# A Trainium2 MLP whose products of two neighbouring weight strips are issued alternately, into four PSUM banks, with the block loop written out

## The chip, the cores and the metric

The kernel runs on one core of a Trainium2 chip. The metric is the device time of one execution in microseconds (us), the median of several runs. The engines are named as in the profile: PE is TensorE (PEld its weight loads), DVE is VectorE, ACT is ScalarE, POOL is GpSimd, SP is SyncE, which here only issues DMAs.

## What is computed

One layer of a streaming encoder over 2048 prompt rows and 32 sample rows of 1024 channels: a normalised input projection, two branches (a recurrence and a banded attention), their merge into x, and then the MLP, which alone is changed. Cut to the MLP, the reference is:

```
D_MODEL = 1024; SEQ = 2048; DEC_SEQ = 32; D_FF = 4 * D_MODEL
...
    h2 = modulate(x, P["norm_mlp_g"][l], sh2, sc2)            # RMS norm, gain and shift
    x = x + g2 * (jnp.square(jax.nn.relu(h2 @ P["w_ff1"][l])) @ P["w_ff2"][l])
...
    y_prompt = rms_norm(xp, final_norm_g)
    y_sample = rms_norm(xs, final_norm_g)
```

All is float32. The kernel splits each float32 factor into a high part (type fp32r, which PE takes in one pass) and the rest, the low part, and adds three products for each: high by high, high weight by low activation, low weight by high activation.

## The kernel before

The stages run one after the other: modulation and first norm, projection and recurrence, attention, merge (`build_merge`), MLP (`build_mlp`). The MLP takes the 2080 rows in NB = 5 blocks of BW = 416 columns; a block is turned so that channels lie on partitions and the 416 rows are the moving columns of every product.

**Units.** A block has 64 units. Unit u uses one weight strip of 1024 by 128 floats (512 KB) and consists of 24 products of 128x128 by 128x416 into one PSUM bank: 8 slices of the contraction by the 3 products named above (`split_products`, L1609). Units 0 to 31 are the first layer: unit u makes 128 of the 4096 hidden channels. Units 32 to 63 are the second layer: output tile m (128 of the 1024 channels) takes four units in a row, q = 0 to 3, all into one bank, m = (u - 32) // 4. The banks `ff_ps0` and `ff_ps1` alternate by u in the first layer and by m in the second.

**Strips.** SP loads strip s into one of four buffers `ff_raw` (L2025) once the low part of strip s - 4 is made. ACT copies it into `ff_hi` (`make_hi`, L2004) once unit s - 2 is through on PE, DVE subtracts that from the strip into `ff_lo` (`make_lo`, L2008), and PE begins the unit when `ff_lo` is there. `ff_hi` and `ff_lo` have two buffers. PE marks a unit as through with the last of its 24 products (semaphore `ff_products`, called `mm_s` in the code).

**What else hangs on a unit.** ACT, DVE and PE each go through the units in the same order; what they do at unit u stands in their `body`, and each engine takes its instructions strictly in that order. In the first layer, once unit u is through, ACT takes the ReLU out of PSUM (L2046), DVE squares it (L2086), ACT and DVE split it (L2051, L2089). In the second layer, once a tile's last unit (q = 3) is through, DVE scales the sum and adds it to x (`x_now`, L2095, two pieces). Between the units stands work for the neighbouring blocks: `final_at(u)` lists the final norm and the output of the block before (squares at units 1 to 8, mean at 10, rows at 12 to 19, transposes and stores at 21, 23, 25, 27), `next_at(u)` the norm of the block that comes next (squares at 35 to 42, mean at 44, the normalised tiles h at 46, 48, ... 60). One tile h is a multiplication on DVE (L1941), the gain and shift and the copy to its high part on ACT (L1927, L1930), and the low part on DVE (L1945).

**The next block's input.** At unit 29 DVE copies the block's input from `x_next` to `x_now` (`move`, L2076, 1.9 us); this stands behind DVE's work on the square of unit 29. SP loads the input of the following block into `x_next` (1664 KB, L1908), and this load stands in SP's program between the loads of strips 32 and 33. It waits for that copy.

**Block loop.** Blocks 0 and 4 are written out; blocks 1 to 3 are a hardware loop (`each_block`, L2010), whose waits compare semaphores with register values.

## Time and profile before

| | us |
|---|---|
| time, median of 3 runs | 5020.41 (5019.88 to 5023.28) |
| span of the profiled execution (first to last instruction), its own time | 5024.5 |
| MLP in the profiled execution, from its first product to its last | 3463.7 to 4991.2 |
| PE busy in the whole span | 4518.3 (90%) |
| DVE, ACT busy in the whole span | 2050.3 (41%), 1480.1 (29%) |
| granted PE clock, mean of the span | 0.935 |

The profile is of one execution, and durations below are its. Matmuls are pipelined on PE and their ends are modelled, so a product's row shows 0.35 us although the next begins after 0.19 us: the distance between the starts of two products is the figure to read, and a unit's length is the distance between the starts of its first product and of the next unit's first. Idle time is shown with the engine and line that ended it.

### The profile page before, as it was taken

To read this page: it belongs to the slowest core of one execution; us is meant where nothing else is said; L and a number is where in the kernel's file an instruction comes from. 1 tells how busy PE (TensorE), PEld (TensorE's weight loads), DVE (VectorE), ACT (ScalarE), POOL (GpSimd) and SP (SyncE) were. 2 spreads that over 40 slices of the span, in tenths; PEclk is the share of its full clock that TensorE was granted. 3 is DMA by queue.
4 is the path that set the end of the run, shared out by engine and by line. 5 is a ranking of instruction groups with operands and counts; after the bars stand their busy time and mean duration, and the time that the engine had idled before them with its cause. 6 is when DMAs were issued, how large, how long until landed. Compare 5 with 4: busy or idle time off the path is not lost. (4 is left out here: it accounts for less than half of the span.)

```text
span 5024.5 us, 69286 instructions
## 1 busy us (share of the span) xinstructions
PE 4518.3 (90%) x25724; PEld 4165.4 (83%) x25724; DVE 2050.3 (41%) x3699; ACT 1480.1 (29%) x2543; POOL 574.0 (11%) x547
## 2 busy tenths in 40 slices
PE   6799899999999999865488878997999999999998
PEld 3599898999999999764366657997999999999997
DVE  3400344444444444443245544333435444353442
ACT  2311222222222222211134333123334344343432
POOL 1210222232222223221000000000000000000000
PEclk9899999999999999977569878998999999999999
DMA  6422111111111111000400004333434434344342
GB/s 223 149 72 69 43 37 38 47 36 36 44 40 36 36 47 37 24 10 7 147 9 8 8 29 156 109 105 102 129 111 118 126 109 137 110 122 123 109 127 81
DMA packets 595632, 390.45 MB, mean 78 GB/s; under 512 B 99313, under 2 KB 585353, under 8 KB 594449
## 3 DMA queue, kind: packets, MB, share of 16 engines
q1 hardware_dynamic: 528336, 309.63, 21.8%
q10 hardware_dynamic: 67136, 78.63, 4.4%
q8 instruction: 109, 1.79, 0.2%
q14 instruction: 51, 0.41, 0.0%
HBM read 306.86 MB, written 81.34 MB: 77 GB/s over the span
## 5 line engine op out<-in xcount | busy, mean ns | idle before, releaser
L522 PE MATMUL proj_ps<-h_hi,w_hi 128*128 128x416 f32 x1680 | 601.2, 358 | 14.8 <-POOL w_lo L507 14.8
L522 PE MATMUL proj_ps<-h_hi,w_lo 128*128 128x416 f32 x1680 | 611.6, 364 | 0.0
L522 PE MATMUL proj_ps<-h_lo,w_hi 128*128 128x416 f32 x1680 | 603.1, 359 | 0.0
L2008 DVE TENSOR_TENSOR ff_lo<-ff_raw,ff_hi 128x1024 fp32r<-128x1024 f32 x320 | 391.5, 1224 | 449.8 <-ACT ff_hi L2004 449.5
L1609 PE MATMUL ff_ps<-h_hi,ff_hi 128*128 128x416 f32 x1280 | 462.9, 362 | 25.5 <-DVE ff_lo L2008 23.9
L2004 ACT ACTIVATE ff_hi<-ff_raw 128x1024 fp32r<-128x1024 f32 x320 | 337.8, 1056 | 454.2 <-PE ff_ps L1609 431.3
L1609 PE MATMUL ff_ps<-hidden_hi,ff_hi 128*128 128x416 f32 x1280 | 459.5, 359 | 3.6 <-DVE ff_lo L2008 3.6
L1609 PE MATMUL ff_ps<-h_hi,ff_lo 128*128 128x416 f32 x1280 | 452.4, 353 | 0.0
L1609 PE MATMUL ff_ps<-hidden_hi,ff_lo 128*128 128x416 f32 x1280 | 451.5, 353 | 0.0
L1609 PE MATMUL ff_ps<-h_lo,ff_hi 128*128 128x416 f32 x1280 | 448.3, 350 | 0.0
L1609 PE MATMUL ff_ps<-hidden_lo,ff_hi 128*128 128x416 f32 x1280 | 447.3, 349 | 0.0
L522 PEld LDWEIGHTS proj_ps<-h_hi,w_hi 128*128 128x128 f32 x1680 | 318.8, 190 | 18.1 <-issue 14.9
L522 PEld LDWEIGHTS proj_ps<-h_lo,w_hi 128*128 128x128 f32 x1680 | 319.0, 190 | 3.8
L522 PEld LDWEIGHTS proj_ps<-h_hi,w_lo 128*128 128x128 f32 x1680 | 318.4, 190 | 4.3
L924 PE MATMUL wkv_two<-solve 128*128 128x128 f32 x2112 | 273.1, 280 | 19.2 <-DVE solve L722 8.0
L924 PEld LDWEIGHTS wkv_two<-solve 128*128 128x128 f32 x2112 | 250.3, 191 | 46.0 <-DVE solve L722 17.7
L1609 PEld LDWEIGHTS ff_ps<-h_hi,ff_hi 128*128 128x128 f32 x1280 | 241.0, 188 | 36.9 <-DVE ff_lo L2008 21.7
L1609 PEld LDWEIGHTS ff_ps<-hidden_hi,ff_hi 128*128 128x128 f32 x1280 | 240.3, 188 | 11.7 <-issue 5.1
L1609 PEld LDWEIGHTS ff_ps<-h_lo,ff_hi 128*128 128x128 f32 x1280 | 241.4, 189 | 8.7 <-issue 5.1
L1609 PEld LDWEIGHTS ff_ps<-hidden_lo,ff_hi 128*128 128x128 f32 x1280 | 240.6, 188 | 8.7 <-issue 5.1
L1609 PEld LDWEIGHTS ff_ps<-h_hi,ff_lo 128*128 128x128 f32 x1280 | 240.7, 188 | 1.9
L1609 PEld LDWEIGHTS ff_ps<-hidden_hi,ff_lo 128*128 128x128 f32 x1280 | 240.0, 188 | 1.8
(288 smaller groups left out, 7666.1 us busy)
## 6 DMA issues: line engine op xcount, KB each, us to landing
ff_raw<-in_w_ff SPq DMA_DIRECT2D x320, 512.0 KB, 4.0
keep_proj<-proj_out ACTq DMA_DIRECT2D x210, 208.0 KB, 1.9
ada_w<-in_w_ada SPq DMA_DIRECT2D x24, 1024.0 KB, 5.8
w_raw<-in_w_in SPq DMA_DIRECT2D x42, 512.0 KB, 4.4
gates<-keep_proj SPq DMA_DIRECT2D x80, 208.0 KB, 2.4
rows_in<-keep_proj SPq DMA_DIRECT2D x32, 448.0 KB, 5.3
x_then_x<-keep_xT SPq DMA_DIRECT2D x40, 208.0 KB, 2.5
keep_x2T<-x_then_x ACTq DMA_DIRECT2D x40, 208.0 KB, 1.9
```

What stands on the lines that cost most here:

```text
L522: mm = pe.matmul(self.ps[u][:, 0:BW], w[:, par, kk, :], a[:, kk, cols], start=(kk == 0 and j == 0), stop=(kk == KD - 1 and j == 2))
L924: mm = pe.matmul(self.bank[bank][:, j * P:(j + 1) * P], lhs[:, j, :], rhs[:, j, :], start=True, stop=True)
L1609: mm = pe.matmul(out, w(i), x(kt), start=(first and i == 0 and j == 0), stop=(last and i == n - 1 and j == 2))
L2004: w.hi_s.done(act.activation(w.whi[:, s % 2], w.raw[:, s % 4], ACT.Copy), s)
L2008: w.lo_s.done(dve.tensor_tensor(w.wlo[:, s % 2], w.raw[:, s % 4], w.whi[:, s % 2].bitcast(F32), ALU.subtract), s)
```

## The change

**Interleaving.** A slot g of PE's program now holds the second half of unit g - 1 (contraction slices 4 to 7) and the first half of unit g (slices 0 to 3), product by product in turn: one of the old unit, one of the new one. Still 24 products stand in a slot; slot 0 and the one after the last unit have 12. The waits of unit g stand at the head of slot g, so also ahead of the second half of unit g - 1. The mark of unit g - 1 is on the last but one product of slot g. The norms' squares and transposes of `next_at` and `final_at` for unit g - 1 stand behind slot g.

**Banks and order of the units.** There are four banks `ff_ps0` to `ff_ps3`. In the second layer the units are taken in pairs of tiles: units 32, 34, 36, 38 are tile 0, units 33, 35, 37, 39 tile 1, and so on (`ff2_unit`), so that neighbouring products always go to different banks. The tiles' last units are 38, 39, 46, 47, 54, 55, 62, 63 (before: 35, 39, 43, ... 63).

**Buffers.** `ff_hi` and `ff_lo` have three buffers instead of two and are made two units ahead in the programs of ACT and DVE instead of one (strip s still waits until the unit that had its buffer, now s - 3, is through); `ff_raw` has three instead of four. To make room, the tile h shares its memory with the output rows `y_rows` (with a wait of DVE for the stores of two blocks before), and the transposed rows have one PSUM tile instead of two.

**Loop.** All five blocks are written out; no wait of the MLP uses a register.

The diff, cut to what is spoken of here:

```diff
+NRAW, NW = 3, 3
...
-        self.raw = sb("ff_raw", [P, 4, KD, P])
-        self.whi, self.wlo = sb("ff_hi", [P, 2, KD, P], F32R), sb("ff_lo", [P, 2, KD, P], F32R)
+        self.raw = sb("ff_raw", [P, NRAW, KD, P])
+        self.whi, self.wlo = sb("ff_hi", [P, NW, KD, P], F32R), sb("ff_lo", [P, NW, KD, P], F32R)
...
+def ff2_unit(u):
+
+    v = u - FF_T
+    return 2 * (v // 8) + v % 2, v % 8 // 2
...
+        def make_hi(act, g):
+            act.wait_ge(w.w_loaded[g % NRAW], 16 * (g // NRAW + 1))
+            if g >= NW:
+                w.mm_s.wait(act, (g - NW) % UNITS, (g - NW) // UNITS + 1)
+            w.hi_s.done(act.activation(w.whi[:, g % NW], w.raw[:, g % NRAW], ACT.Copy), g % UNITS)
...
-            body(0, 1, False, True)
-            with eng.Fori(1, NB - 1) as b:
-                body(b, b + 1, True, True)
-            body(NB - 1, NB, True, False)
+            for b in range(NB):
+                body(b, b + 1, b > 0, b < NB - 1)
...
                     for s in range(UNITS):
-                        w.lo_s.wait(sp, s - 4, turn) if s >= 4 else w.lo_s.wait(sp, UNITS + s - 4, turn - 1)
-                        sp.dma_start(w.raw[:, s % 4], w.strip(s)).then_inc(w.w_loaded[s % 4], 16)
+                        g = nth(s, turn)
+                        if g >= NRAW:
+                            w.lo_s.wait(sp, (g - NRAW) % UNITS, (g - NRAW) // UNITS + 1)
+                        sp.dma_start(w.raw[:, g % NRAW], w.strip(s)).then_inc(w.w_loaded[g % NRAW], 16)
                         if s == FF_T and after:
                             next_sync(sp, b + 1, turn + 1)
...
                     for u in range(UNITS):
-                        if u + 1 < UNITS:
-                            make_lo(dve, u + 1, turn)
-                        elif after:
-                            make_lo(dve, 0, turn + 1)
+                        if nth(u, turn) + 2 < NB * UNITS:
+                            make_lo(dve, nth(u, turn) + 2)
...
-                        if u >= FF_T and u % 4 == 3:
-                            m = (u - FF_T) // 4
+                        if u >= FF_T and ff2_unit(u)[1] == 3:
+                            m = ff2_unit(u)[0]
                             w.mm_s.wait(dve, u, turn)
...
+                for g in range(NB * UNITS + 1):
+                    now, old = (g % UNITS, g // UNITS + 1), ((g - 1) % UNITS, (g - 1) // UNITS + 1)
+                    if g < NB * UNITS:
+                        begin(*now)
+                    for kt in range(HALF):
+                        for j in range(3):
+                            if g > 0:
+                                product(*old, HALF + kt, j)
+                            if g < NB * UNITS:
+                                product(*now, kt, j)
+                    if g > 0:
+                        besides(*old)
```

`begin` holds the unit's waits, `product` is one matmul (j = 0, 1, 2 for the three products) and sets the mark with a unit's last one, `besides` holds the squares and transposes.

How the instructions stand on three engines follows. In these lists `h2` is the tile that the profile calls `h`, `x3` is the semaphore of the copy and of the finished tiles of x, `next_norm` and `next_affine` are those of the tiles h, and the digit behind `ff_ps` is the bank.

PE where unit 1 begins, before:

```order
L1609 MATMUL ff_ps0<-h2_hi,ff_lo 128x416
L1609 MATMUL ff_ps1<-h2_hi,ff_hi 128x416 [waits x3,ff_lo_made]
L1609 MATMUL ff_ps1<-h2_lo,ff_hi 128x416
L1609 MATMUL ff_ps1<-h2_hi,ff_lo 128x416
L1609 MATMUL ff_ps1<-h2_hi,ff_hi 128x416
```

and now:

```order
L2161 MATMUL ff_ps0<-h2_hi,ff_hi 128x416 [waits x3,ff_lo_made]
L2161 MATMUL ff_ps1<-h2_hi,ff_hi 128x416
L2161 MATMUL ff_ps0<-h2_lo,ff_hi 128x416
L2161 MATMUL ff_ps1<-h2_lo,ff_hi 128x416
L2161 MATMUL ff_ps0<-h2_hi,ff_lo 128x416
L2161 MATMUL ff_ps1<-h2_hi,ff_lo 128x416
```

The wait for unit 1's strip has moved ahead of the second half of unit 0, and the bank changes with every product.

SP from the MLP's start to the loads behind unit 32 of block 0, before:

```order
L1908 DMA x_next<-keep_x2T 128x8x416 [waits x3]
L2025 DMA ff_raw<-in_w_ff1 128x8x128 [waits ff_lo_made] x32
L2025 DMA ff_raw<-in_w_ff2 128x8x128 [waits ff_lo_made]
L1908 DMA x_next<-keep_x2T 128x8x416 [waits x3]
L2025 DMA ff_raw<-in_w_ff2 128x8x128 [waits ff_lo_made] x31
```

and now:

```order
L1915 DMA x_next<-keep_x2T 128x8x416 [waits x3]
L2039 DMA ff_raw<-in_w_ff1 128x8x128 x3
L2039 DMA ff_raw<-in_w_ff1 128x8x128 [waits ff_lo_made] x29
L2039 DMA ff_raw<-in_w_ff2 128x8x128 [waits ff_lo_made]
L1915 DMA x_next<-keep_x2T 128x8x416 [waits x3]
L2039 DMA ff_raw<-in_w_ff2 128x8x128 [waits ff_lo_made] x31
```

The load of the next block's input keeps its place between strips 32 and 33, with the strips behind it; the mark of unit 29, from which its wait follows, now comes with slot 30.

DVE around the first tile h (unit 46) of block 0, before:

```order
L1936 RECIPROCAL norms<-norms 128x416 [waits next_rms]
L2008 TENSOR_TENSOR ff_lo<-ff_raw,ff_hi 128x1024 [waits ff_hi_made] x2
L1941 TENSOR_TENSOR h2<-x_next,norms 128x416 [waits next_norm]
L2008 TENSOR_TENSOR ff_lo<-ff_raw,ff_hi 128x1024 [waits ff_hi_made]
L2095 SCALAR_TENSOR_TENSOR x_now<-ff_ps1,modulation,x_now 128x384 [waits ff_products]
L2095 SCALAR_TENSOR_TENSOR x_now<-ff_ps1,tail_now,x_now 128x32
```

and now:

```order
L1943 RECIPROCAL norms<-norms 128x416 [waits next_rms]
L2022 TENSOR_TENSOR ff_lo<-ff_raw,ff_hi 128x1024 [waits ff_hi_made] x2
L2106 SCALAR_TENSOR_TENSOR x_now<-ff_ps2,modulation,x_now 128x384 [waits ff_products]
L2106 SCALAR_TENSOR_TENSOR x_now<-ff_ps2,tail_now,x_now 128x32
L1950 TENSOR_TENSOR h2_or_y_rows<-x_next,norms 128x416 [waits next_norm]
L2022 TENSOR_TENSOR ff_lo<-ff_raw,ff_hi 128x1024 [waits ff_hi_made]
```

The tile h of unit 46 now stands behind the addition of a tile whose last unit is 46, and so behind that unit's mark; the same holds at unit 54.

## Rows read from the trace of the kernel before

**Rows 1.** The page, part 1: busy us, share of the span, instructions.
```profile
PE 4518.3 (90%) x25724; PEld 4165.4 (83%) x25724; DVE 2050.3 (41%) x3699; ACT 1480.1 (29%) x2543; POOL 574.0 (11%) x547
```

**Rows 2.** Windows: stretch, length, busy us and count by engine, PE clock, DMA.
```profile
400.00:450.00 50.00, 50.00 (x267) 49.49 (x266) 0.00 (x0) 7.99 (x14) 4.80 (x2) 1.00 0.20 68
...
3480.00:4990.00 1510.00, 1499.49 (x7856) 1458.49 (x7855) 668.15 (x829) 569.21 (x817) 0.00 (x0) 1.00 0.41 119
...
4850.00:4900.00 50.00, 50.00 (x267) 49.55 (x266) 15.21 (x16) 11.66 (x11) 0.00 (x0) 1.00 0.40 117
```

**Rows 3.** Waits from 3440 us on: total us, times, longest us.
```profile
PE ff_ps L1609 <- DVE ff_lo L2008: 27.5, 14, 18.6
```

**Rows 4.** Timeline of PE: start, us, instruction; first products of units 47 to 49, then a norm.
```profile
3994.60 0.35 PE L1609 MATMUL ff_ps<-hidden_hi,ff_hi 128*128 128x416 f32 x1
...
3999.13 0.35 PE L1609 MATMUL ff_ps<-hidden_hi,ff_hi 128*128 128x416 f32 x1
...
4003.66 0.35 PE L1609 MATMUL ff_ps<-hidden_hi,ff_hi 128*128 128x416 f32 x1
...
4101.80 0.35 PE L1609 MATMUL ff_ps<-h_hi,ff_lo 128*128 128x416 f32 x1
4101.99 0.86 PE L1984 MATMUL norm_ps<-squares,ones 128*128 128x416 f32 x2
```

**Rows 5.** Timelines around unit 33 of block 1: PE (units 30, 31, 33), DVE, SP, ACT.
```profile
3910.02 0.35 PE L1609 MATMUL ff_ps<-h_hi,ff_hi 128*128 128x416 f32 x1
...
3915.01 0.45 PE L1609 MATMUL ff_ps<-h_hi,ff_hi 128*128 128x416 f32 x1 [0.30 <-DVE ff_lo L2008]
...
3925.23 0.47 PE L1609 MATMUL ff_ps<-hidden_hi,ff_hi 128*128 128x416 f32 x1 [0.90 <-DVE ff_lo L2008]
...
3911.86 1.89 DVE L2076 COPY x_now<-x_next 128x3328 f32<-128x3328 f32 x1
...
3913.91 0.38 SPq L1908 DMA_DIRECT2D x_next<-keep_x2T  x1
3914.41 13.04 SPq L2025 DMA_DIRECT2D ff_raw<-in_w_ff  x6
...
3922.86 1.06 ACT L2004 ACTIVATE ff_hi<-ff_raw 128x1024 fp32r<-128x1024 f32 x1 [2.06 <-DMA ff_raw<-in_w_ff]
...
3923.95 1.23 DVE L2008 TENSOR_TENSOR ff_lo<-ff_raw,ff_hi 128x1024 fp32r<-128x1024 f32 x1 [2.47 <-ACT ff_hi L2004]
```

**Rows 6.** Timelines of DVE and ACT around the first tile h of block 1.
```profile
3992.50 0.58 DVE L1941 TENSOR_TENSOR h<-x_next,norms 128x416 f32<-128x416 f32 x1
...
3993.12 0.71 ACT L1927 ACTIVATE h<-h,modulation,gain_mlp 128x384 f32<-128x384 f32 x1 [1.80 <-DVE h L1941]
...
3994.80 1.06 ACT L2004 ACTIVATE ff_hi<-ff_raw 128x1024 fp32r<-128x1024 f32 x1
...
3995.89 1.23 DVE L2008 TENSOR_TENSOR ff_lo<-ff_raw,ff_hi 128x1024 fp32r<-128x1024 f32 x1 [2.81 <-ACT ff_hi L2004]
...
3999.33 0.62 DVE L2095 SCALAR_TENSOR_TENSOR x_now<-ff_ps,modulation,x_now 128x384 f32<-128x384 f32 x1 [2.21 <-PE ff_ps L1609]
3999.86 0.24 DVE L2095 SCALAR_TENSOR_TENSOR x_now<-ff_ps,tail_now,x_now 128x32 f32<-128x32 f32 x1
```

**Rows 7.** Timeline of PE where the loop turns from block 1 to block 2.
```profile
4071.47 0.35 PE L1609 MATMUL ff_ps<-hidden_hi,ff_lo 128*128 128x416 f32 x1
...
4072.53 0.45 PE L1609 MATMUL ff_ps<-h_hi,ff_hi 128*128 128x416 f32 x1 [0.71 <-issue]
```

**Rows 8.** PE after idle time: a wait in the merge and its window, the MLP's first unit.
```profile
3156.41 0.45 PE L1609 MATMUL merge_pso<-merged_hi,merge_w_hi 128*128 128x416 f32 x1 [2.59 <-DVE merged_lo L1768]
...
3158.00:3161.40 3.40, 3.40 (x11) 3.24 (x11) 0.00 (x0) 0.00 (x0) 0.00 (x0) 0.51 0.00 0
...
3463.70 0.71 PE L1609 MATMUL ff_ps<-h_hi,ff_hi 128*128 128x416 f32 x1 [18.59 <-DVE ff_lo L2008]
...
3470.53 0.35 PE L1609 MATMUL ff_ps<-h_hi,ff_hi 128*128 128x416 f32 x1
```

More of the change, by code:

```diff
@@ L1836, in __init__ @@
         self.nrm = sb("norms", [P, BW])
-        self.h = sb("h2", [P, 2, BW])
-        self.yo = sb("y_rows", [P, D])
+        self.yo = sb("h2_or_y_rows", [P, D])
+        self.h = self.yo[:, 0:2 * BW].rearrange("p (a t) -> p a t", t=BW)
         self.cur = sb("tail_now", [P, 2, 24])
         self.ones = sb("ones", [P, P])
-        self.ps = [ctx.enter_context(nc.psum_tensor(f"ff_ps{j}", [P, 512], F32)) for j in range(2)]
+        self.ps = [ctx.enter_context(nc.psum_tensor(f"ff_ps{j}", [P, 512], F32)) for j in range(4)]
         self.pn = [ctx.enter_context(nc.psum_tensor(f"norm_ps{j}", [P, 512], F32)) for j in range(2)]
-        self.pt = [ctx.enter_context(nc.psum_tensor(f"rows_ps{j}", [P, D], F32)) for j in range(2)]
-        self.w_loaded = [sem(f"ff_loaded{j}") for j in range(4)]
+        self.pt = ctx.enter_context(nc.psum_tensor("rows_ps", [P, D], F32))
+        self.w_loaded = [sem(f"ff_loaded{j}") for j in range(NRAW)]
         self.x_loaded = sem("x2_loaded")
@@ L1918, in next_act @@
                 w.n_pe.wait(act, KD - 1, turn)
-                if not isinstance(turn, int) or turn > 1:
+                if turn > 1:
                     w.f_dve.wait(act, KD - 1, turn - 2)
@@ L1938, in next_dve @@
                 w.n_dve.wait(dve, "rstd", turn)
+                if j == 0 and turn > 2:
+                    dve.wait_ge(w.y_stored, 64 * (turn - 2))
                 if j >= 2:
@@ L1961, in final_act @@
                 w.f_pe.wait(act, KD - 1, turn)
-                w.n_dve.wait(act, ("lo", KD - 1), min(turn + 1, NB) if isinstance(turn, int) else turn + 1)
+                w.n_dve.wait(act, ("lo", KD - 1), min(turn + 1, NB))
                 w.f_rms.done(act.activation(w.nrm[:, :], w.pn[1][:, 0:BW], ACT.Sqrt, scale=1.0 / D, bias=k.eps[:, 0:1]), "rms")
@@ new lines, in bank, with begin @@
+                def bank(u):
+                    return w.ps[u % 4] if u < FF_T else w.ps[ff2_unit(u)[0] % 4]
+                def begin(u, turn):
+                    w.lo_s.wait(pe, u, turn)
+                    if u < FF_T:
+                        if u == 0:
+                            w.n_dve.wait(pe, ("lo", KD - 1), turn)
+                        if u >= 4:
+                            w.relu_s.wait(pe, u - 4, turn)
+                        else:
+                            w.x_s.wait(pe, 4 + u, turn - 1)
+                    else:
+                        m, q = ff2_unit(u)
+                        if q == 0:
+                            if m < 4:
+                                w.relu_s.wait(pe, FF_T - 4 + m, turn)
+                            else:
+                                w.x_s.wait(pe, m - 4, turn)
+                        if m == 0:
+                            w.ulo_s.wait(pe, 8 * q + 7, turn)
@@ new lines, in product @@
+                def product(u, turn, kt, j):
+                    q = 0 if u < FF_T else ff2_unit(u)[1]
+                    whi, wlo = w.whi[:, nth(u, turn) % NW, kt, :], w.wlo[:, nth(u, turn) % NW, kt, :]
+                    xhi, xlo = (w.hhi[:, kt, :], w.hlo[:, kt, :]) if u < FF_T else (w.uhi[:, 8 * q + kt, :], w.ulo[:, 8 * q + kt, :])
+                    mm = pe.matmul(bank(u)[:, 0:BW], wlo if j == 2 else whi, xlo if j == 1 else xhi,
+                                   start=(q == 0 and kt == 0 and j == 0), stop=((u < FF_T or q == 3) and kt == KD - 1 and j == 2))
+                    if kt == KD - 1 and j == 2:
+                        w.mm_s.done(mm, u)
@@ L2151, in _, with besides @@
+                def besides(u, turn):
+                    if turn > 1:
+                        for part, j in for_tensor(w.final_at, u):
+                            final_pe(pe, part, j, turn - 1)
+                    if turn < NB:
+                        for part, j in for_tensor(w.next_at, u):
+                            next_pe(pe, part, j, turn + 1)
                 for part, j in FIRST:
                     next_pe(pe, part, j, 1)
-                each_block(pe, body)
+                HALF = KD // 2
```

68 lines of the change are left out of this document (19 added, 49 removed).

## The prediction, made before the changed kernel ran

> **What bounds the kernel now.** I read the page first: PE is busy for 90% of the span [rows 1]. The windows then show that the MLP is more extreme: of the 1510 us from 3480 on PE is busy for 1499, at full granted clock, with one weight load for each product, while DVE and ACT stand at 44% and 38% [rows 2]. So the MLP's time is the number of products times their distance, plus what PE waits. The distance comes from the starts of units [rows 4]: 3994.60, 3999.13, 4003.66, which is 4.53 us for 24 products or 188.9 ns each. The waits are few: PE waited 27.5 us in all for a strip's low part, 18.6 of it once at the start of the MLP [rows 3]; by the timeline the other 13 are five behind the copy to x_now (unit 31), four behind the final norm's mean (unit 12) and four at unit 33 of blocks 0 to 3. A change here can gain by a shorter distance or by taking these waits away, and it loses by every new wait, since nothing else lies on the path.
>
> **Part by part.** Durations are those of the profiled execution (span 5024.5 us, 0.08% above the median of 5020.41); the sum is a difference and is set on the median.
>
> **Distance of the products: 0.** The shape row says 416 columns; at 2.4 GHz, the level that a granted clock of 1.00 stands for [rows 2], these take 173.3 ns, so 15.6 ns of each product are something else. If that were a cost of writing the same bank twice running, it would have to be missing wherever the bank changes. Unit 47 ends tile 3 and unit 48 begins tile 4 in the other bank: 4.53 us. Units 48 and 49 share a bank: 4.53 us [rows 4]. A difference of 15 ns would show in rows of 10 ns. A start flag that happens to cost what the bank saves is no way out: between a product and the norm's product (other bank) lie the same 0.19 us [rows 4]. The other thing the interleaving alters is which operands follow each other: today high by high and high by low share their weights, afterwards neighbours never do. But loads equal products in number, 7855 for 7856 [rows 2], so no load is saved today. Which addresses are read together does not matter much either: the projection, with other tensors in other places, puts 267 products into 50 us, and so does the MLP [rows 2]. One product more or less in 267 is 0.7 ns each, so for 7680 products I take 0 and keep -5.5 to +5.5 us.
>
> Here a rule speaks for the change. The Trainium skill, "TensorE: Matmul & The Clock Gate", section "Back-to-back issue gap", gives N/2.4 + 2.5 ns for the distance at full clock, an estimate of 175.8 ns for 416 columns; the trace has 188.9. If alternation brought the products down to that rule, 7680 x 13.1 ns or 101 us would go, where the rows make it 0.
>
> **Marks one product earlier, loop written out: -2.9 us.** The mark of an old unit is on the last but one product of its slot, so what follows it starts 0.19 us sooner against the next slot. Making strip halves keeps its place otherwise: the third buffer gives one slot, and a unit now spans two. So the waits at unit 12 (four) and behind the copy (the one of block 4; the others are in the next term) stay, each 0.19 shorter: -1.0. The loop turns twice; there PE's distance is 1.06 us in place of 0.19 [rows 7]: -0.87 each, with the 0.1 that the first products after a stop lose (0.31 in place of 0.19), -1.9. Blocks 0 and 4 are straight code already and show the same unit length, so the longer program costs nothing I can see.
>
> **The load behind unit 32: +17.4 us.** This is the largest term. In SP's program the next block's input stands ahead of strip 33 and waits for DVE's copy, which waits for the mark of unit 29. That mark now comes at the end of slot 30, one slot later, while strip 33 is still wanted at the head of slot 33. In block 1 [rows 5]: unit 30 starts (mark of 29) at 3910.02, copy 3911.86, the 1664 KB load 3913.91, strip 33 issued 3914.41 behind it, its high part at 3922.86 after ACT waited 2.06 for the DMA, low part 3923.95, unit 33 at 3925.23, PE idle 0.90. So from the mark to unit 33 it is 15.21 us. It is already the last to end, and there is no slack. Afterwards slot 30 takes 4.53 us without a wait, and 15.21 - 0.19 later slot 33 can begin: 19.55 from the start of unit 30 where it was 15.21, +4.34. Four blocks have a next one: +17.4. PE then stands still for about 5.6 us at the head of slot 33, with the second half of unit 32 queued behind the wait. The 1664 KB and strip 33, 2176 KB together, arrived in 8.95 us, so strip 34 should follow some 2.1 us later and has a whole slot. I see nothing that would catch the stop up; if strip 34 were late by its 2.1 us too, four times that would add 8.4, which is the upper end.
>
> **PE's clock after that stop: +6.0 us.** In the merge an idle time of 2.59 us was followed from 3158.0 to 3161.4 by a window at 0.51 with 11 products at 0.35 us distance [rows 8]; 18 would fit, so 1.5 us were lost. At the MLP's start, after 18.59 us, the first unit took 6.83 us in place of 4.53: 2.3 lost [rows 8]. A stop of 5.6 us lies between the two; nearer to the first, so 4 x 1.5. Ends: 0 and 4 x 2.3 = 9.2.
>
> **Tile additions ahead of h: +8.0 us.** Today the tiles' last units are odd and h is made at even ones. Afterwards units 46 and 54 have both, and DVE's multiplication for h stands behind an addition that waits for the unit's mark. The way from the mark [rows 5, 6]: addition at 3999.33, 0.20 after unit 48's start, so 0.01 after the slot's end with the earlier mark; second piece +0.53; h about +0.2; ACT's gain +0.62; the next strip's high part, which stands behind h on ACT, +1.68; low part +1.09; PE +1.28. Together 5.41 us where a slot has 4.53: 0.9 and 0.1 for the restart, twice in each of four blocks. Today h is made early in its unit and the same chain ends in time. Ends: half and one and a half times, 4 to 12.
>
> The other edits I cost at 0: the single PSUM tile for the output rows and the memory shared by h and y_rows add waits for things that lie a slot or more back, and three strip buffers leave a strip more than 9 us from issue until ACT wants it, against the 8.5 of the slowest in rows 5.
>
> **Sum:** 0 - 2.9 + 17.4 + 6.0 + 8.0 = +28.5; 5020.4 + 28.5 = 5049 us, +0.57%. With the ends: 28.5 - 5.5 - 6.0 - 4.0 = +13 to 28.5 + 5.5 + 3.2 + 4.0 + 8.4 = +50, 5033 to 5070.
>
> **Rivals.**
> Same-bank cost (faster): the 15.6 ns belong to two products running into one bank and vanish only when neighbours alternate throughout. 7680 x 15.6 = 120 us less; 5049 - 120 = 4929. For it speaks only that these ns have no name in the profile; against it the equal units and the equal distance before a norm [rows 4]. By the rule above the same rival ends at 5049 - 101 = 4948. The strip's late arrival and h would not fill this up. From 2.4 ns per product on (18 us) the sum would fall under the 0.2% line.
>
> Strip 33 comes in time (no change): if the queue serves the strip beside the 1664 KB instead of behind them, or the copy is not held by the mark as I read it, the stop and the clock's fall go: 5049 - 17.4 - 6.0 = 5025. Against it: 8.4 us from issue to the high part today [rows 5], with the strips behind it following.
>
> Clock swinging (slower): were PE to pause a little at each change of bank, half-clock stretches would come within units, 1.5 us each [rows 8]; one in every tenth unit would be 48 us, 5097. The clock is 1.00 over 1510 us, with a change of bank at every unit of the first layer [rows 2], so this is unlikely. The Trainium skill has such a case, same page, "A second HAM failure mode: psum-queue depth-cycling": a kernel that cycles through PSUM banks and whose clock goes up and down. No stretch of this MLP shows it.
>
> **How the numbers follow.** The forecast has 0.75, same-bank cost 0.10, strip in time 0.12, clock swinging 0.03. Faster or slower by 0.2% (10 us) is about what a measurement of this kernel tells from no change. The forecast's whole range (+13 to +50) lies above that line: slower 0.78 with the swinging clock; no change 0.12; faster 0.10. The range takes the forecast and the strip that comes in time with its 5.5 us below, 5019, and ends at 5070; the two others are left out.
>
> **What would show it.** Unit starts still 4.53 us apart in quiet stretches of the second layer. Slot 33 of blocks 0 to 3 some 10 us long with PE idle 5 to 6 us until ff_lo, ACT's high part before it ended by the DMA, and a window near 0.5 behind it. Slots 48 and 56 of the same blocks some 5.5 us, ended by ff_lo. Block edges without the 1.06. A distance of 176 ns, or no long stop at slot 33, would prove me wrong; so would stops at strips elsewhere, which would point to the third strip buffer.

## The result and the profile after

The changed kernel takes **5051.34 us** in the median (5048.81 to 5055.51, 4 runs), the kernel before 5020.28 (5019.88 to 5023.28) beside it: ratio **1.0059**, 95% interval 1.0045 to 1.0073. That is slower by 0.59%. Predicted were 5049 us and a range of 5019 to 5070.

PE is as busy as before (4519.7 us in the page's part 1, 4518.3 in [rows 1]), so the added time is idle time and time at a lower clock. The windows of the MLP after, with the same columns as [rows 2]: the stretch is 25 us longer, PE's busy time only 2.6, and the mean granted clock has fallen from 1.00 to 0.99. The second row is 3.4 us behind a stop of PE in block 1: clock 0.50, 10 products where 18 would fit.

```profile
3480.00:5015.00 1535.00, 1502.12 (x7845) 1461.11 (x7843) 664.52 (x829) 566.57 (x815) 0.00 (x0) 0.99 0.40 116
3931.50:3934.90 3.40, 3.33 (x10) 3.22 (x11) 2.65 (x5) 1.10 (x2) 0.00 (x0) 0.50 0.68 191
```

The waits from 3440 us on (total us, times, longest us) name who is waited for: PE's waits for `ff_lo` have gone from 27.5 us [rows 3] to 50.0, and ACT's waits for a strip to land from 11.1 us in eight, the longest 2.2, to 31.0 in four, the longest 8.5. ACT before, then PE and ACT after:

```profile
ACT ff_hi L2004 <- DMA ff_raw<-in_w_ff: 11.1, 8, 2.2
...
PE ff_ps L2161 <- DVE ff_lo L2022: 50.0, 17, 18.6
ACT ff_hi L2018 <- DMA ff_raw<-in_w_ff: 31.0, 4, 8.5
```

The four stand at one place, once in each of blocks 0 to 3. Here are the timelines around slot 33 of block 1: PE (slots 30 and 32, the last product before the stop, slot 33 and the clock's return), DVE, SP, ACT. Each line answers to one of [rows 5].

```profile
3912.18 0.53 PE L2161 MATMUL ff_ps<-h_hi,ff_hi 128*128 128x416 f32 x2
...
3921.42 0.45 PE L2161 MATMUL ff_ps<-h_hi,ff_hi 128*128 128x416 f32 x1
...
3925.88 0.35 PE L2161 MATMUL ff_ps<-hidden_hi,ff_lo 128*128 128x416 f32 x1
3931.57 1.06 PE L2161 MATMUL ff_ps<-hidden_hi,ff_hi 128*128 128x416 f32 x2 [5.34 <-DVE ff_lo L2022]
3932.43 0.90 PE L2161 MATMUL ff_ps<-hidden_lo,ff_hi 128*128 128x416 f32 x2
...
3936.14 0.54 PE L2161 MATMUL ff_ps<-hidden_lo,ff_hi 128*128 128x416 f32 x2
...
3918.35 1.89 DVE L2089 COPY x_now<-x_next 128x3328 f32<-128x3328 f32 x1
...
3930.29 1.22 DVE L2022 TENSOR_TENSOR ff_lo<-ff_raw,ff_hi 128x1024 fp32r<-128x1024 f32 x1 [7.42 <-ACT ff_hi L2018]
...
3920.26 0.37 SPq L1915 DMA_DIRECT2D x_next<-keep_x2T  x1
3920.68 13.37 SPq L2039 DMA_DIRECT2D ff_raw<-in_w_ff  x5
...
3929.20 1.06 ACT L2018 ACTIVATE ff_hi<-ff_raw 128x1024 fp32r<-128x1024 f32 x1 [7.02 <-DMA ff_raw<-in_w_ff]
```

Slot 30 starts at 3912.18. The copy begins 6.17 us later (1.84 in [rows 5], and a slot of 4.51 less the 0.19 of the earlier mark), the load is issued behind it, strip 33 behind the load, and it lands 8.5 us after its issue as before. PE gets to slot 33 at 3931.57, 19.39 us after slot 30's start, where it was 15.21. Then two products (one row of x2) take 0.7 us, until 3935.8; later 0.38.

The second place is an addition with h behind it. Timelines of PE, DVE and ACT at slot 48 of block 1, answering to [rows 6]:

```profile
4007.05 0.53 PE L2161 MATMUL ff_ps<-hidden_hi,ff_hi 128*128 128x416 f32 x2
...
4012.23 0.64 PE L2161 MATMUL ff_ps<-hidden_hi,ff_hi 128*128 128x416 f32 x2 [0.50 <-DVE ff_lo L2022]
...
4007.06 0.62 DVE L2106 SCALAR_TENSOR_TENSOR x_now<-ff_ps,modulation,x_now 128x384 f32<-128x384 f32 x1 [2.14 <-PE ff_ps L2161]
...
4007.75 0.58 DVE L1950 TENSOR_TENSOR h_or_y_rows<-x_next,norms 128x416 f32<-128x416 f32 x1
4010.95 1.23 DVE L2022 TENSOR_TENSOR ff_lo<-ff_raw,ff_hi 128x1024 fp32r<-128x1024 f32 x1 [2.62 <-ACT ff_hi L2018]
...
4008.37 0.71 ACT L1934 ACTIVATE h_or_y_rows<-h_or_y_rows,modulation,gain_mlp 128x384 f32<-128x384 f32 x1 [4.71 <-DVE h_or_y_rows L1950]
...
4009.88 1.04 ACT L2018 ACTIVATE ff_hi<-ff_raw 128x1024 fp32r<-128x1024 f32 x1
```

h is now made 0.7 us after the slot's start, behind the addition; the strip's high part stands behind it on ACT (4009.88), its low part ends at 4012.2, and the slot lasts 5.18 us.

At the block edge the 1.06 us of [rows 7] are gone, 0.20 is left (PE, first slot of block 2):

```profile
4080.85 0.35 PE L2161 MATMUL ff_ps<-hidden_hi,ff_hi 128*128 128x416 f32 x1
4081.05 0.35 PE L2161 MATMUL ff_ps<-h_hi,ff_hi 128*128 128x416 f32 x1
```

**The account.** I took the lengths of all units before and all slots after (distance of their first products) and what each exceeds its kernel's quiet unit or slot by (4.533 and 4.515 us; quiet is one that holds no wait and no product of a norm). A stop at the head of slot 33 is thereby in the length of slot 32. First to last product of the MLP: 1527.5 us before, 1552.7 after, +25.2.

| term, us | predicted | before | after | difference |
|---|---|---|---|---|
| quiet length x 320 | 0 | 4.5331 | 4.5148 | -5.9 |
| stalls of unit 12, and of the copy in block 4 | -1.0 | 5.6 | 4.6 | -1.0 |
| loop turns | -1.9 | 2.1 | 0.0 | -2.1 |
| units 30 to 32, blocks 0 to 3 (the load) | +17.4 | 6.4 | 26.3 | +19.9 |
| slot 33, blocks 0 to 3 (the clock) | +6.0 | 0.5 | 8.5 | +8.0 |
| slots 48, 49, 56, 57 (h) | +8.0 | 0.0 | 6.2 | +6.2 |
| first unit, and the rest (norms, transposes) | 0 | 62.5 | 62.6 | +0.1 |
| sum | +28.5 | | | +25.2 |

Ahead of the MLP the profiled execution after was 2.9 us faster, behind its last product it was 2.4 slower (2.1 of that one slow store of output rows, which no other run of an interleaved kernel below had; 0.3 is left of the single PSUM tile for the rows). So the spans differ by 24.6. The medians differ by 31, since the span of the kernel before, 5024.5 us, is 4 us above its median and that of the kernel after, 5049.1, 2 below; in the later comparisons the median of the kernel before was 5023 to 5026. Below I therefore take ratios from runs on the same chip, and for single terms the MLP's length from first to last product in the trace.

### The profile page after: what moved, and what is told of

Its sections match the earlier page's. It is cut to its first block and busy times, and to the rows that moved or that the text cites. A ratio compares the mean times of both kernels' runs of the same rounds, so it can differ in the third digit from the quotient of the medians.

```text
span 5049.1 us, 68124 instructions
## 1 busy us (share of the span) xinstructions
PE 4519.7 (90%) x25724; PEld 4169.6 (83%) x25724; DVE 2047.7 (41%) x3699; ACT 1479.7 (29%) x2543; POOL 573.9 (11%) x547
## 5 line engine op out<-in xcount | busy, mean ns | idle before, releaser
L2161 PE MATMUL ff_ps<-hidden_hi,ff_hi 128*128 128x416 f32 x1280 | 363.5, 363 | 28.4 <-DVE ff_lo L2022 28.4
L2161 PE MATMUL ff_ps<-h_hi,ff_hi 128*128 128x416 f32 x1280 | 361.7, 361 | 21.9 <-DVE ff_lo L2022 21.7
L2161 PE MATMUL ff_ps<-hidden_lo,ff_hi 128*128 128x416 f32 x1280 | 352.1, 354 | 0.0
L2161 PE MATMUL ff_ps<-h_lo,ff_hi 128*128 128x416 f32 x1280 | 350.3, 352 | 0.0
L2161 PE MATMUL ff_ps<-hidden_hi,ff_lo 128*128 128x416 f32 x1280 | 349.3, 352 | 0.0
L2161 PE MATMUL ff_ps<-h_hi,ff_lo 128*128 128x416 f32 x1280 | 347.8, 350 | 0.0
L2161 PEld LDWEIGHTS ff_ps<-h_hi,ff_hi 128*128 128x128 f32 x1280 | 238.7, 188 | 37.3 <-DVE ff_lo L2022 25.7
```

Source lines behind the costliest of these rows:

```text
L2161: mm = pe.matmul(bank(u)[:, 0:BW], wlo if j == 2 else whi, xlo if j == 1 else xhi, start=(q == 0 and kt == 0 and j == 0), stop=((u < FF_T ...
```

## The experiments

My theory: the added time is (1) the stop at slot 33 because strip 33 stands behind the load in SP's program, with PE's clock after it, and (2) h behind the addition; the interleaving itself costs nothing. Rivals: three strip buffers are too few; the interleaving has a price of its own; and, for the 0.8 ns that a product did get shorter, the bank against the order of the operands. In the table, MLP is the way from its first to its last product and quiet the mean length of a quiet unit or slot, both from the trace of one execution.

| kernel | median, us | ratio to before, 95% | MLP, us | quiet, us |
|---|---|---|---|---|
| before | 5020 to 5026 | | 1527.5 | 4.533 |
| after | 5051.34 | 1.0059 (1.0045 to 1.0073) | 1552.7 | 4.515 |
| e1_load_behind_35 | 5015.43 | 0.9986 (0.9977 to 0.9995) | 1520.0 | 4.516 |
| e2_h_first | 5044.16 | 1.0048 (1.0035 to 1.0060) | 1548.3 | 4.518 |
| e3_both | 5008.99 | 0.9973 (0.9964 to 0.9983) | 1513.5 | 4.518 |
| e4_load_behind_33 | 5021.47 | 0.9994 (0.9985 to 1.0003) | 1528.3 | 4.515 |
| e12_load_from_act | 5013.02 | one run | 1520.2 | 4.517 |
| e7_before_load_moved | 5016.49 | 0.9987 (0.9979 to 0.9996) | 1521.4 | 4.533, block 0's first units 4.507 |
| e8_before_moved_unrolled | 5019.40 | 0.9986 (0.9977 to 0.9995) | 1519.5 | 4.533 |
| e5_same_bank | 5008.95 | 0.9966 (0.9953 to 0.9978) | 1513.8 | 4.518 |
| e6_halves_in_turn | 5012.21 | 0.9970 (0.9958 to 0.9982) | 1512.9 | 4.533 |
| e9_halves_slices_alternate | 5001.49 | 0.9950 (0.9936 to 0.9963) | 1502.6 | 4.507 |
| e10_units_slices_alternate | 5007.94 | 0.9964 (0.9950 to 0.9978) | 1510.7 | 4.507 |
| e11_units_weights_apart | 5014.95 | 0.9977 (0.9967 to 0.9986) | 1520.4 | 4.533 |

### The load moved: e1_load_behind_35

```diff
-                        if s == FF_T and after:
+                        if s == FF_T + 3 and after:
                             next_sync(sp, b + 1, turn + 1)
```

> The kernel after, with the next block's input loaded behind strip 35 instead of behind strip 32 in SP's program; nothing else is changed. Theory (strip 33 queued behind the 1664 KB load makes the stop): the four stops go, which the trace of after puts at 19.8 us from the start of slot 30 to that of slot 33, and with them the half-clock stretch behind each, 8.4 us: 5051.3 - 28.2 = 5023 us (5020 to 5026); slots 32 and 33 of blocks 0 to 3 are 4.51 us, and ff_hi no longer waits for the DMA. Rival 1 (three strip buffers are too few, whatever stands in front): a stop remains at the strip that now stands behind the load, number 36, some 10 us long, and the time stays at 5045 to 5051. Rival 2 (the stop is only where a wait for DVE's copy shows): the time stays within 3 us of 5051.

The stops are gone: slots 32 and 33 of block 1 start at 3914.41, 3919.03 and (34) 3923.55, so they last 4.62 and 4.52 us, and PE's waits for `ff_lo` fall to 25.7 us. Starts, then waits:

```profile
3914.41 0.45 PE L2161 MATMUL ff_ps<-h_hi,ff_hi 128*128 128x416 f32 x1
...
3919.03 0.35 PE L2161 MATMUL ff_ps<-hidden_hi,ff_hi 128*128 128x416 f32 x1
...
3923.55 0.35 PE L2161 MATMUL ff_ps<-hidden_hi,ff_hi 128*128 128x416 f32 x1
```

```profile
PE ff_ps L2161 <- DVE ff_lo L2022: 25.7, 13, 18.6
```

The time fell further than I had written, to 5015 and not 5023, and 5.2 of these 8 us are an error in my sum: I took away the stop's excess over the kernel before (19.9), but the repaired kernel also loses what the kernel before paid at this place. In the trace units 30 to 32 go from 26.3 to 1.3 and slot 33 from 8.5 to 0: 33.4 us, not 28.2. The rest lies between executions: the MLP is 32.7 us shorter, the medians 36. Rival 1 falls: strip 36, now the one behind the load, takes 7.7 to 8.5 us to land and nothing waits for it, so three strip buffers suffice once the load stands behind a strip that isn't wanted so soon.

### Half of that: e4_load_behind_33

The diff is that of e1_load_behind_35 with `FF_T + 1`.

> The kernel after, with the next block's input behind strip 33 instead of strip 32: half of the repair, to test the arithmetic. Theory: strip 34 now arrives 8.5 us (blocks 1 and 2) or 10.0 us (blocks 0 and 3) after the load's issue, but is wanted one slot later: unit 34 can start 8.5 + 2.4 us after 3920.7 in block 1, 1.3 us after the end of an undisturbed slot 33, and 2.8 us in blocks 0 and 3: stops of 8.2 us in all where there were 19.8. If stops this short cost no clock, the time is 5023 + 8 = 5031 us; if each is followed by a half-clock stretch of 1.5 us, 5037. Rival (the stop does not depend on which strip stands behind the load): 5051.

Against e1_load_behind_35 the MLP is 8.3 us longer, where I had 8.2 without a loss of clock; that the two agree is luck. The stops at the head of slot 34 add 1.1 and 1.0 us in blocks 1 and 2 and 2.4 and 2.6 in blocks 3 and 0 (expected 1.3 and 2.8), 7.0 in all, and 1.7 come from the clock in block 3. The absolute time is 10 us under the 5031, 5.2 of them by the error above. Unexpected is the clock. The starts of slot 34 in blocks 0 and 3, and the 3.4 us behind them:

```profile
3618.21 0.65 PE L2161 MATMUL ff_ps<-hidden_hi,ff_hi 128*128 128x416 f32 x2 [2.39 <-DVE ff_lo L2022]
...
4544.19 0.64 PE L2161 MATMUL ff_ps<-hidden_hi,ff_hi 128*128 128x416 f32 x2 [2.24 <-DVE ff_lo L2022]
```

```profile
3618.20:3621.60 3.40, 3.39 (x18) 1.00 0.56 170
4544.20:4547.60 3.40, 3.40 (x11) 0.59 0.57 171
```

Behind 2.39 us of idle time the granted clock stayed at 1.00 with 18 products in the window; behind the shorter 2.24 it was 0.59 with 11, and the slot lost 1.7 us. The length of the stop alone does not decide. The merge, which is the same code in all fourteen kernels, says so more often: it has four waits of 2.5 to 2.6 us, and of these 56 in the traces 31 cost 1.4 to 1.7 us, by distance of products, with a clock of 0.52 to 0.73 in the 3.4 us behind them (all four in the kernel before, [rows 8]), and 25 cost 0.1 at 1.00 (all four in e1_load_behind_35). The wait of [rows 8] and its window in e1_load_behind_35:

```profile
3161.00 0.45 PE L1609 MATMUL merge_pso<-merged_hi,merge_w_hi 128*128 128x416 f32 x1 [2.59 <-DVE merged_lo L1768]
...
3161.00:3164.40 3.40, 3.40 (x18) 1.00 0.24 77
```

The stops of 5.3 to 6.8 us in the MLPs of the kernel after and of e2_h_first were all eight followed by 0.50. What decides behind the short ones is open.

### h ahead of the addition: e2_h_first and e3_both

```diff
+                        if after:
+                            for part, j in w.next_at(u):
+                                if part == "h":
+                                    next_dve(dve, part, j, turn + 1, b + 1)
                         if u >= FF_T and ff2_unit(u)[1] == 3:
...
                             for part, j in w.next_at(u):
-                                next_dve(dve, part, j, turn + 1, b + 1)
+                                if part != "h":
+                                    next_dve(dve, part, j, turn + 1, b + 1)
```

> The kernel after, with DVE's multiplication for a tile h placed ahead of the tile addition at the units that have both (46 and 54); nothing else is changed. Theory (h waits behind the addition, which waits for the unit's mark): slots 48, 49, 56 and 57 of blocks 0 to 3 fall from 5.18 and 4.63 to 4.51 us, 0.78 us eight times: 5051.3 - 6.2 = 5045 us. Rival (DVE or ACT is short of time there whatever their order): the slots keep their 5.18, or a slot next to them takes the stall over, and the time stays at 5051.

> The kernel after with both edits: the next block's input behind strip 35, and h ahead of the addition. Theory: both gains are independent, 5051.3 - 28.2 - 6.2 = 5017 us, 3 us below the kernel before, so within 0.2% of it (ratio 0.9985 to 1.0005): the interleaving itself then costs nothing and gives at most the 0.8 ns by which its products lie closer, 6 us. Rival (the interleaving has a price of its own that no single slot shows): 5025 us or more.

Slots 48 and 49 of block 1 in e2_h_first are 4.52 us each, by their starts and that of slot 50; all sixteen such slots together exceed a quiet one by 0.03 us instead of 6.2.

```profile
4002.68 0.35 PE L2166 MATMUL ff_ps<-hidden_hi,ff_hi 128*128 128x416 f32 x1
...
4007.20 0.35 PE L2166 MATMUL ff_ps<-hidden_hi,ff_hi 128*128 128x416 f32 x1
...
4011.72 0.35 PE L2166 MATMUL ff_ps<-hidden_hi,ff_hi 128*128 128x416 f32 x1
```

5044.2 us fits the 5045 of the theory. The MLP of this trace is only 4.4 us shorter than after the change: h gave its 6.2, but the half-clock stretches behind the four stops cost 9.8 us in place of 8.5, and its quiet slots are 4.518 us in place of 4.515, 1 us in all. With both edits the kernel is *faster* than before, 0.9973, below my 0.9985 to 1.0005, mostly by the error in the sum of e1_load_behind_35; by the trace the two gains add up (1552.7 - 33.4 - 6.2 = 1513.1, measured 1513.5). That leaves no room for a hidden price of the interleaving; what it does inside a quiet slot makes that shorter, not longer.

### The fair counterpart: e7_before_load_moved and e8_before_moved_unrolled

The kernel before with the diff of e1_load_behind_35, and with its block loop written out as well.

> The kernel before, with the next block's input loaded behind strip 35 instead of behind strip 32, nothing interleaved: the fair counterpart of e1_load_behind_35 and e3_both. Theory: the waits at unit 33 of blocks 0 to 3 go (units 32 and 33 last 5.47 to 5.70 and 4.61 to 4.67 us where a quiet one has 4.53): 4.6 us less, ratio 0.9991. Rival (the load in its new place holds up a strip of the kernel before, which has four strip buffers and loads one strip further ahead): 1.0000 or more, with a wait at unit 36 or 37.

> The kernel e7_before_load_moved with the block loop written out as in the change, products still unit by unit. Theory: the two turns of the loop go, 2.1 us by the units at the block edges: ratio 0.9987. The length of a quiet unit says whether the written-out program is what brings the products closer: 4.533 by the theory (it is the alternation), 4.515 by the rival (6 us less, ratio 0.9975). Compared with e3_both, 0.9973, this kernel leaves what the interleaving alone is worth: some 7 us by the theory, 1 by the rival.

The load cost the kernel before 4.6 us at units 30 to 33 (6.4 + 0.5 of excess, 2.3 + 0.0 afterwards), and no wait has come up at units 36 or 37. The MLP is 6.1 us shorter; 0.5 of that is in its first unit and 0.8 in something that I had not looked for. First products of units 4, 29 and 31 of block 0, and of units 50 and 62 of block 4, in e7_before_load_moved:

```profile
3475.98 0.35 PE L1609 MATMUL ff_ps<-h_hi,ff_hi 128*128 128x416 f32 x1
...
3588.64 0.35 PE L1609 MATMUL ff_ps<-h_hi,ff_hi 128*128 128x416 f32 x1
...
3598.06 0.46 PE L1609 MATMUL ff_ps<-h_hi,ff_hi 128*128 128x416 f32 x1 [0.25 <-DVE ff_lo L2008]
...
4914.23 0.35 PE L1609 MATMUL ff_ps<-hidden_hi,ff_hi 128*128 128x416 f32 x1
...
4968.63 0.35 PE L1609 MATMUL ff_ps<-hidden_hi,ff_hi 128*128 128x416 f32 x1
```

112.66 / 25 = 4.506 us for a unit until PE waits 0.25 us at unit 31, and 54.40 / 12 = 4.533 afterwards: one program, one order of products, two distances. This matters for the next two sections.

Written out (e8), the block edges lose 1.9 us in the trace, which the times (0.9987 and 0.9986) don't resolve, and the quiet unit is 4.533. Against it e3_both is 6.0 us shorter in the MLP: this is what the interleaving with its banks, buffers and order of units is worth, where 7 were expected. The times, 0.9973 and 0.9986, have intervals that overlap.

### Why the products lie closer: e5_same_bank and e6_halves_in_turn

Both are e1_load_behind_35 with one edit. e5 takes the bank's change out of the second layer, e6 the alternation out of the slot.

```diff
 def ff2_unit(u):
...
-    return 2 * (v // 8) + v % 2, v % 8 // 2
+    return v // 4, v % 4
```

```diff
                             if g > 0:
                                 product(*old, HALF + kt, j)
+                    for kt in range(HALF):
+                        for j in range(3):
                             if g < NB * UNITS:
                                 product(*now, kt, j)
```

> The kernel e1_load_behind_35, with the second layer's units again in the order of the kernel before (four units of one tile in a row): alternating products of the second layer then go to the same bank three quarters of the time, while their operands still alternate. The first layer keeps its two banks. What is asked is where the 0.8 ns come from by which the products lie closer after the change (a slot of 24 is 4.515 us where a unit was 4.533). Theory (the order of the operands): slots of the second layer stay at 4.515, as those of the first. Rival (the change of bank): slots of the second layer go back to 4.533, the first layer's stay at 4.515; 2.4 us for the kernel. The tiles' last units are odd again, so the h term must go as well: 48, 49, 56 and 57 of blocks 0 to 3 at a quiet slot's length, 6.2 us less than e1_load_behind_35, a ratio to the kernel before of 0.9973.

> The kernel e1_load_behind_35, with the two halves of a slot one after the other (twelve products of the old unit, then twelve of the new one) instead of product by product: banks change twice in a slot, and high by high and high by low share their weights as in the kernel before. Theory (it is the alternation that brings the products closer): slots of 24 at 4.533 us again, 320 x 0.018 = 6 us more. Rival (it is the written-out program, the four banks or the buffers): they stay at 4.515. The old unit's mark now comes in the middle of its slot, 2.26 us earlier, so under both the waits of slots 48, 49, 56, 57 and those of slots 12 and 13 go (6.2 + 4.2 us) and half of those of slots 31 and 32. Ratio to the kernel before: 0.9977 by the theory, 0.9965 by the rival.

First products of slots 4 and 29 of block 0 (25 slots) in e6_halves_in_turn, then of slots 50 and 62 of block 4 (12 slots, second layer) in e5_same_bank:

```profile
3480.91 0.35 PE L2161 MATMUL ff_ps<-h_hi,ff_hi 128*128 128x416 f32 x1
...
3594.24 0.35 PE L2161 MATMUL ff_ps<-h_hi,ff_hi 128*128 128x416 f32 x1
```

```profile
4910.84 0.35 PE L2161 MATMUL ff_ps<-hidden_hi,ff_hi 128*128 128x416 f32 x1
...
4965.07 0.35 PE L2161 MATMUL ff_ps<-hidden_hi,ff_hi 128*128 128x416 f32 x1
```

113.33 / 25 = 4.533 us: without the alternation the gain is gone, though the banks change twice in each slot. 54.23 / 12 = 4.519: with the alternation, in one bank, it is there; slots of the kernels with alternating banks are 4.513 or 4.520 from stretch to stretch. So the alternating order gives it and not the bank; the time of e6, 0.9970, lies between theory and rival and would not have told. In e6 the mark of a unit comes half a slot earlier, and the stalls of unit 12 and of h are gone as expected, that of the copy wholly where I had half.

### The order without units: e9, e10, e11

e9_halves_slices_alternate is e6_halves_in_turn, e10_units_slices_alternate and e11_units_weights_apart are e8_before_moved_unrolled, each with another order of the products. e9 and e10 alternate between two slices of one unit, e11 keeps a slice's three products together but parts the two that share a weight tile. e9 against e6, for each half of a slot:

```diff
-                    for kt in range(HALF):
-                        for j in range(3):
+                    for i in range(HALF // 2):
+                        for j in range(3):
+                            for kt in (2 * i, 2 * i + 1):
```

e10 and, behind it, e11, in a copy of `split_products` that the MLP alone calls:

```diff
-    for i, kt in enumerate(kts):
-        for j, (w, x) in enumerate(((hi, x_hi), (hi, x_lo), (lo, x_hi))):
+    turns = [(i + d, j) for i in range(0, len(kts), 2) for j in range(3) for d in (0, 1)]
```

```diff
-        for j, (w, x) in enumerate(((hi, x_hi), (hi, x_lo), (lo, x_hi))):
+    products = ((hi, x_lo), (lo, x_hi), (hi, x_hi))
```

> The kernel e6_halves_in_turn (all twelve products of the old unit, then twelve of the new one; its slots were 4.533 us), but within each half the products of two contraction slices of the same unit alternate: neighbours then go to the same bank nearly throughout, and no two neighbours share a weight or an activation tile. Theory (operands that differ bring the products closer, whatever the bank): quiet slots 4.513 to 4.520 us, and 320 x 0.016 = 5 us less than e6_halves_in_turn, while the waits at slots 12, 31 and 48 stay away: MLP about 1508 us from first to last product, ratio to the kernel before 0.996. Rival (it needs the interleaving of two units): slots at 4.533, ratio 0.997.

> The kernel e8_before_moved_unrolled (units one after the other, two banks, two buffers; units of 4.533 us), with the products of two contraction slices of a unit alternating: three lines, no interleaving of units. Theory (operands): a quiet unit 4.513 to 4.520 us, 5 us less than e8_before_moved_unrolled, ratio 0.9975. Rival (it needs two units or two banks): 4.533, ratio 0.9986.

> The kernel e8_before_moved_unrolled with the three products of each slice in another order: high weight by low activation, low by high, high by high. Neighbours then never share a weight tile, but the second and third share the activation tile. Theory 1 (what costs is a weight tile loaded twice running): units as short as in e10_units_slices_alternate, 4.513 to 4.520 us. Theory 2 (what costs is an activation tile read twice running): the before order shares none between neighbours except across no boundary, so the units would be longer than 4.533 us. If neither sharing matters but the distance to the next use of the bank or slice does, 4.533.

First products of units 4 and 29 of block 0, in e10_units_slices_alternate and then in e11_units_weights_apart:

```profile
3486.03 0.35 PE L1903 MATMUL ff_ps<-h_hi,ff_hi 128*128 128x416 f32 x1
...
3598.70 0.35 PE L1903 MATMUL ff_ps<-h_hi,ff_hi 128*128 128x416 f32 x1
```

```profile
3479.84 0.35 PE L1903 MATMUL ff_ps<-h_lo,ff_hi 128*128 128x416 f32 x1
...
3593.17 0.35 PE L1903 MATMUL ff_ps<-h_lo,ff_hi 128*128 128x416 f32 x1
```

112.67 / 25 = 4.507 us against 113.33 / 25 = 4.533. Two slices that alternate within one unit, in one bank, give more (1.1 ns per product) than the change got with two units and four banks (0.8), and a little more than the 4.513 to 4.520 that I expected. That settles what suffices for the gain; why, it does not.

e11 came out as neither of its theories: it parts the two products that share a weight tile, sets two that share an activation tile side by side, and nothing moves. In ns, averaged over the 25 units, the distances repeat every six products, that is every two slices: 187.6, 183.3, 190.8, 190.0, 189.2, 192.4 in the kernel before, and the same within 0.1 in e11, each at its place in the row whatever its operands are. So sharing a tile with the neighbour, of weights or of activations, is not the cause. In e10 the six are 192.4, 185.9, 182.4, 188.3, 188.4, 189.2.

And the order doesn't set the distance outright: in the ten quiet stretches that I took in each trace (units 4 to 29 or 14 to 20 of the first layer, 50 to 62 or 58 to 62 of the second, in five blocks), the orders that keep a slice's three products together (before, e6, e7, e8, e11) are at 4.533 in 49 of 50, but once, in e7, at 4.507, with six others again: 185.0, 189.2, 184.1, 195.0, 190.0, 183.4. The alternating order of e9 and e10 is at 4.507 in all 20, that of the change and its descendants at 4.513 or 4.520 in every one. It looks as if a stream fell into a rhythm at its start and kept it until the next wait, and the order decided which rhythms are likely; this is argued from these counts and rows, and no run shows how it comes about.

e9_halves_slices_alternate has the lowest time here: 0.9950 (expected 0.996), 25 us less in the MLP than before, with one wait of PE for `ff_lo` left, that for the first strip:

```profile
PE ff_ps L2161 <- DVE ff_lo L2022: 18.6, 1, 18.6
```

By the account its 25 us are 8.4 from the distance, 7.4 from the load and the copy (units 30 to 33), 5.1 from unit 12 and 2.1 from the loop; the rest is in the first unit and the norms. Besides the change's banks, buffers and order of units it keeps of the interleaving only that a unit spans two slots, for the earlier mark. e10_units_slices_alternate, which has none of these, is 2.8 us shorter in the MLP than e3_both, the change with both repairs; their times (0.9964 and 0.9973) don't resolve that.

### Another queue: e12_load_from_act

```diff
-                        if s == FF_T and after:
-                            next_sync(sp, b + 1, turn + 1)
...
+                        if after and u == 30:
+                            next_sync(act, b + 1, turn + 1)
```

> The kernel after, with the next block's input loaded by ACT behind its work on unit 30 instead of by SP; SP's strips no longer stand behind a wait for the copy. Theory (strip 33 is late because it stands behind the load in SP's program): the stops at slot 33 go and the time falls to that of e1_load_behind_35, about 5015 us. Rival (the 1664 KB take the engines' time from whichever strip comes next): a stop remains at the strip that is issued just behind the load, 35, with its high part waiting for the DMA. The strip that follows the load by a microsecond also tells whether a second queue is served beside the first: it lands after 3 to 6 us if it is, after some 8.5 if the transfers come in the order of issue.

5013.0 us in its one run, and the MLP is as long as that of e1_load_behind_35 (1520.2 and 1520.0). Strip 33 now comes because it is issued before the load, not because of the second queue. The issues around the load in block 1 (KB each, us to landing):

```profile
x_next<-keep_x2T ACTq DMA_DIRECT2D x1, 1664.0 KB, 9.0
ff_raw<-in_w_ff SPq DMA_DIRECT2D x1, 512.0 KB, 9.2
```

Strip 35, issued 0.16 us behind the load on the other queue, takes 9.2 us, and the load 9.0; in the four blocks the strip takes 9.0 to 10.4 and the load 8.8 to 10.2. On one queue, in the kernel after, the load took 7.1 to 8.6 and the strip behind it 8.5 to 10.0. Neither of my two numbers (3 to 6, and 8.5) was right: a strip behind the load gains nothing by a queue of its own, and the load loses. The Trainium skill, "DMA: Bandwidth & Descriptors", section "Issuing engines are not separate DMA queues", says that transfers started by different engines run on the same 16 DMA engines and interleave; this trace agrees, with the two landing 0.3 to 0.4 us apart, where on one queue the strip landed 1.8 us behind the load.

## Why the prediction was right

**Right** were the sign, the likeliest case and its mechanism: of +25.2 us in the MLP the load and the clock behind it make 27.9, h 6.2, and e1_load_behind_35, e2_h_first and e3_both took away each by itself. The chain from slot 30 to slot 33 came out as worked from [rows 5], 19.39 us for 19.55 in blocks 1 and 2. That the sum came so near is in part luck: the load and the clock were 4.5 us too low, h and the distance 7.7 too high.

**The load, +17.4, measured +19.9.** The mis-sized part is one assumption: that block 1 stands for all. In blocks 0 and 3 strip 33 landed 10.0 us after its issue, not 8.5, and the way from slot 30 was 20.9 us. The rows of before could not tell: there it took 8.4 to 8.5 in all four blocks. Why it is later in these two is open. The upper end that I had for such lateness (8.4) covers it.

**The clock, +6.0, measured +8.0.** The four stretches lost 2.4, 1.9, 1.7 and 2.5 us. I took the loss from the idle time of 2.59 us in the merge [rows 8]; the one behind 18.59, 2.3, was the nearer row. A wait of that length is followed by a loss in 31 of 56 cases and by none in 25 (above), so the row was also of the costly kind by chance.

**h, +8.0, measured +6.2.** The chain was right link by link; I counted 5.41 us for 5.18, above all in ACT's step from the gain to the strip's high part, 1.68 by [rows 6] and 1.51 here.

**Marks and loop, -2.9, measured -3.1.**

**Distance, 0, measured -5.9.** This step failed, though within 0.4 us of its lower end. The bank was judged rightly, and the four equal distances of [rows 4] were the right rows: e5_same_bank shows no cost of the bank, and the 101 us by the rule of the Trainium skill ("TensorE: Matmul & The Clock Gate", section "Back-to-back issue gap") did not come; a product takes 188.1 ns here and 187.8 at best, not 175.8. That section gives the formula for an isolated product, which the prediction left out. Wrong was the next step, that the order of the operands does not matter because as many weights are loaded and the projection is as fast. The projection runs its products at the distance that the MLP before has, so it could show that other addresses change nothing, but not what another order does. No row of before shows an alternating order, and the term should have had a range for that.

**The rivals.** Strip 33 in time did not occur, nor did the clock swing without a stop: in quiet slots it is 1.00. Same-bank cost is refuted by e5_same_bank. What I had said would show the forecast is there but for the quiet slots, which are 4.515 us and not 4.53, with the stop of 10.1 to 11.6 us counted, by distance of first products, to slot 32, and its half-clock stretch to slot 33.

## What to carry to other kernels

A change that delays one mark by a slot must be followed to every queue in which something waits for that mark: here the mark of unit 29, a copy, a load, and the strip that happened to stand behind the load cost 28 us, and moving the load by three places in one program gives them back and more. Where a stream of products is the bound, try alternating two contraction slices before banks and units are rearranged; it is a few lines, and it gave 1.1 ns of 188.9 here. And a repaired stall is worth its whole length, also the part that the kernel before had paid.

## What the runs showed of the hardware beyond that

The mean distance of products has levels (187.8, 188.1, 188.3 and 188.9 ns) that hold for a whole stretch; which one it is goes with the order in which two slices' products are issued, at equal counts of products and weight loads and within one bank (e10_units_slices_alternate), but one program showed two of them (e7_before_load_moved). The cause is open. A stop of 2.24 us was followed by a stretch at clock 0.59 and one of 2.39 us by full clock (e4_load_behind_33), and the merge's four waits of 2.5 to 2.6 us cost some 6 us in one execution (before) and 0.5 in another (e1_load_behind_35) with the same code. A 512 KB strip issued just behind a 1664 KB load takes 8.5 to 10 us on the same queue (after) and 9.0 to 10.4 on another (e12_load_from_act), where the median strip takes 4.1.
